# A transformer layer on one core: attention in even steps, token loads in small pieces

## What is computed

```python
h = x @ w_in                                  # split into q, k, v, z, b, a, c_q, c_kv, k_r
o_gdn = gated_delta_rule(q, k, v, g, beta)    # chunks of 64 tokens, 4 heads
for blk in range(S // Q_BLOCK):               # attention, 4 heads, keys up to the end of the block
    s = (einsum(q_nope, k_nope) + einsum(q_rope, k_rope)) * scale
    prob = softmax(where(mask, s, -inf))
    out = einsum(prob, v)
mix = concat([o_gdn, o_mla]) @ w_out
x = layer_norm(ALPHA * x + mix)
x = layer_norm(ALPHA * x + (silu(gate) * up) @ w_down)       # gate, up = split(x @ w_gate_up)
return x + sigmoid(x @ w_ple_gate) * (p_i @ w_ple)
```

## Time and profile before

| | us |
|---|---|
| median of 3 runs | 3401.8 (3395.01 to 3408.82) |
| the profiled execution, its time | 3407.16 |
| its span, first to last instruction | 3405.7 |
| attention, first matmul to the end of its last | 1101.6 to 1511.1 |
| op stage, first w_hi copy to the first matmul of feed_in | 1516.1 to 1744.6 |
| TensorE busy in the span | 3095.6 (91%) |
| mean granted TensorE clock | 0.958 |

### The profile page before, as it was taken

One profiled execution on the slowest core, in us unless ns is written; L12 is line 12 of the kernel. 1 busy time (PEld: TensorE's weight loads), 2 busy tenths in 40 slices (PEclk: granted clock), 3 DMA queues, 4 the chain that ended last, 5 costly groups with the idle time before them and its releaser, 6 DMA issues. The chain is left out here.

```text
span 3405.7 us, 45425 instructions
## 1 busy us (share of the span) xinstructions
PE 3095.6 (91%) x15074; PEld 2550.6 (75%) x15074; DVE 1641.7 (48%) x2713; ACT 1064.9 (31%) x2363; POOL 1115.6 (33%) x1245
## 2 busy tenths in 40 slices
PE   6999997768887897979879999989998999999898
PEld 5888885557776776868667888878887788887676
DVE  3653005446664554555576545675554433333333
ACT  2111004334434554542233333433333311111321
POOL 2322241165655866620045333453332000000122
PEclk9999998889988998999989999999999999999999
DMA  3212115412223211125624222232221532333433
GB/s 142 78 74 79 69 62 188 157 51 80 70 61 98 60 41 52 30 73 181 220 84 136 74 92 74 75 114 92 74 90 53 176 101 88 101 96 116 150 120 97
DMA packets 284042, 329.32 MB, mean 97 GB/s; under 512 B 32896, under 2 KB 224256, under 8 KB 279552
## 3 DMA queue, kind: packets, MB, share of 16 engines
q1 hardware_dynamic: 238248, 265.84, 24.6%
q0 software_dynamic: 12384, 45.09, 3.8%
q10 hardware_dynamic: 33280, 16.78, 1.7%
HBM read 210.73 MB, written 116.92 MB: 96 GB/s over the span
## 5 line engine op out<-in xcount | busy, mean ns | idle before, releaser
L2107 PE MATMUL ff_bank<-ff_x_hi,ff_w_lo 128*128 128x512 f32 x1240 | 488.2, 394 | 31.9 <-DVE ff_w_lo L2287 22.5
L2108 PE MATMUL ff_bank<-ff_x_lo,ff_w_hi 128*128 128x512 f32 x1240 | 487.0, 393 | 0.0
L2109 PE MATMUL ff_bank<-ff_x_hi,ff_w_hi 128*128 128x512 f32 x1240 | 486.6, 392 | 0.0
L2090 POOL TENSOR_TENSOR ff_w_sum<-ff_w_raw 128x512 f32<-128x512 f32 x210 | 299.3, 1435 | 495.7 <-DVE ff_w_lo L2287 439.3
L299 PE MATMUL in_h_ps<-in_x_hi,in_w_lo 128*128 128x512 f32 x704 | 276.6, 393 | 26.0 <-POOL in_w_lo L255 26.0
L2107 PEld LDWEIGHTS ff_bank<-ff_x_hi,ff_w_lo 128*128 128x128 f32 x1240 | 235.6, 190 | 84.0 <-DVE ff_w_lo L2287 25.3
L2497 PE MATMUL fd_acc<-fd_w_hi,fd_a_lo 128*128 128x512 f32 x704 | 279.8, 397 | 13.2 <-DVE fd_a_lo L2481 13.2
L2499 PE MATMUL fd_acc<-fd_w_hi,fd_a_hi 128*128 128x512 f32 x704 | 278.0, 395 | 0.0
L2498 PE MATMUL fd_acc<-fd_w_lo,fd_a_hi 128*128 128x512 f32 x704 | 278.0, 395 | 0.0
L301 PE MATMUL in_h_ps<-in_x_hi,in_w_hi 128*128 128x512 f32 x704 | 275.8, 392 | 0.0
L300 PE MATMUL in_h_ps<-in_x_lo,in_w_hi 128*128 128x512 f32 x704 | 275.8, 392 | 0.0
(11 more groups left out here) (383 smaller groups left out, 6640.6 us busy)
## 6 DMA issues: line engine op xcount, KB each, us to landing
ff_w_raw<-w_gate_up SPq DMA_DIRECT2D x44, 1024.0 KB, 5.1
scratch_hT<-in_out SPq DMA_DIRECT2D x22, 1024.0 KB, 3.9
fd_a_raw<-scratch_hid SPq DMA_DIRECT2D x176, 128.0 KB, 2.1
dr_qkv<-scratch_hT SPq DMA_DIRECT2D x16, 768.0 KB, 5.2
in_w_raw<-w_in POOLq DMA_DIRECT2D x22, 512.0 KB, 3.9
scratch_hid<-ff_first SPq DMA_DIRECT2D x44, 256.0 KB, 2.3
scratch_hid<-ff_second SPq DMA_DIRECT2D x44, 256.0 KB, 2.3
fd_w_raw<-w_down SPq DMA_DIRECT2D x22, 512.0 KB, 5.3
```

The lines of the kernel that those rows point to most:

```text
L2090: pool.tensor_tensor(w_sum[:, SUM_SLOT[m]], w_raw[:, b, one], w_raw[:, b, two], op).then_inc(w_sum_done, 1)
L2107: pe.matmul(acc, w_lo[:, wm, ws], x_hi[:, xm, k], start=first_mm, stop=False, skip_group_check=skip)
L2108: pe.matmul(acc, w_hi[:, wm, ws], x_lo[:, xm, k], start=False, stop=False, skip_group_check=skip)
L2109: return pe.matmul(acc, w_hi[:, wm, ws], x_hi[:, xm, k], start=False, stop=last_mm, skip_group_check=skip)
```

## The change

Attention is written without a loop, as 144 steps, one for each pair. Blocks of a head come in the order j = 7, 0, 6, 1, 5, 2, 4, 3. In step (n, p) TensorE transposes the pair two further on, also across blocks, multiplies pair p with v, and then does a share of the score groups of block n+3: of its G groups, those from G·p/pairs to G·(p+1)/pairs. Three blocks' scores are made before the first step. Four buffers of probabilities take the place of two (two of them half as long), three score banks the place of four, and two accumulators the place of one. The next head's pieces come at fixed steps, from step 2 to step 20 of a head; VectorE now copies the high part (`split_highs`, 60 copies in all: 36 single and 12 twice) and GpSimd makes the low part only. `HIGH_AT` puts the first head's last five pieces at the end of `delta_rule`.

```diff
+    ORDER = [j for m in range(NB // 2) for j in (NB - 1 - m, m)]
+    blocks = [(h, j) for h in range(HEADS) for j in ORDER]
+    LOOK, AHEAD = 3, 2
+    S_RING, T_RING, ACCS = 3, 3, 2
+    FIRST_PIECE, PIECE_STEPS = 2, 20
...
+        def steps():
+            every = [(n, p) for n in range(N) for p in range(pairs[n])]
+            for i, (n, p) in enumerate(every):
+                upto = min(i + AHEAD + 1, len(every))
+                turns, n_turned = every[n_turned:upto], upto
+                now, m = [], n + LOOK
+                if m < N:
+                    all_m = score_groups(m)
+                    now = all_m[len(all_m) * p // pairs[n]:len(all_m) * (p + 1) // pairs[n]]
...
+            for n, p, turns, now, ends, whole, left, pieces in steps():   # TensorE
+                for n1, p1 in turns:
+                    turn(n1, p1)
+                values(n, p)
+                for group in now:
+                    scores(*group)
...
+                if kind == 2:                                             # VectorE, split_highs
+                    reached(dve, split_low, count + 1 - 4)
+                    dve.tensor_copy(qr_hi[:], src)
+                    dve.tensor_copy(qr[b][ROPE:, ts], src[ROPE:]).then_inc(split_high, 1)
+                else:
+                    dve.tensor_copy((q_hi, k_hi, None, v_hi)[kind][b][:, ts], src).then_inc(split_high, 1)
...
+            for n, p, turns, now, ends, whole, left, pieces in steps():   # VectorE
+                for n1, p1 in turns:
+                    low(n1, p1)
+                if whole is not None:
+                    scales(whole)
+                for group in now:
+                    maximum(*group)
+                for h, m in pieces:
+                    split_highs(h, m)
+                if ends is not None:
+                    gaps(ends)
```

The token loads of the feed stage come as 16 pieces of 256 KB in place of four of 1 MB, both in the op stage and between the two passes of `feed_in`. In the op stage a weight load goes behind the first chunk load of tile 10 and of tile 11, and one token piece behind each chunk load of tiles 12 to 15:

```diff
+    def prepare_feed(sp, tp, t, c):
+        piece = tp.CH * (t - TILES) + c + 16
+        if piece >= 0:
+            feed_load_x(sp, ff, x1T, 0, piece)
+        elif c == 0:
+            sp.wait_ge(tp.w_lo_done, tp.K)
+            feed_load_w(sp, ff, a["w_gate_up"], t % 2, t % 2)
```

More of the change, by code:

```diff
@@ L1615, in attention @@
         out_done = s.sem("out_done")
-        out_free = s.sem("out_free")
-        stored = s.sem("stored")
+        stored = [s.sem(f"stored{b}") for b in range(2)]
         block = ctx.enter_context(nc.Block())
[L1619 to L1630, removed]
         def widths(j, tile):
@@ new lines, in steps @@
+        def steps():
+            every = [(n, p) for n in range(N) for p in range(pairs[n])]
+            n_turned, whole, left, count = 0, None, None, 0
+            for i, (n, p) in enumerate(every):
[5 more added lines that the diff above has]
+                    now = all_m[len(all_m) * p // pairs[n]:len(all_m) * (p + 1) // pairs[n]]
+                ends = m if m < N and p + 1 == pairs[n] else None
+                h, i0 = blocks[n][0], pair0[NB * blocks[n][0]]
+                pieces = [m for m in range(PIECES) if h + 1 < HEADS and i0 + FIRST_PIECE + PIECE_STEPS * m // PIECES == i]
+                yield n, p, turns, now, ends, whole, left, [(h + 1, m) for m in pieces]
+                whole, left = ends, n if p + 1 == pairs[n] else None
@@ L1748, in values @@
                 last.then_inc(pv_done, 1)
[L1750 to L1766 removed]
+            pe.wait_ge(const_sem, 2)
@@ L1768, in _ @@
+            for n in range(LOOK):
+                for group in score_groups(n):
+                    scores(*group)
[4 more added lines that the diff above has]
+                for group in now:
+                    scores(*group)
         @block.scalar
         def _(act):
[L1770 to L1778 removed]
@@ new lines, in out_copy @@
+            def out_copy(n):
+                act.wait_ge(pv_done, pair0[n + 1])
+                reached(act, stored[n % 2], 16 * (n // 2))
+                act.activation(out[:, n % 2], acc_ps[:, n % ACCS, 0:QB], ACT.Copy).then_inc(out_done, 1)
+            act.preload_act_table(ACT.Exp)
+            for n in range(LOOK):
+                for group in score_groups(n):
+                    exps(*group)
+                factors(n)
+            for n, p, turns, now, ends, whole, left, pieces in steps():
+                if left is not None:
+                    out_copy(left)
+                for n1, p1 in turns:
+                    high(n1, p1)
+                for group in now:
+                    exps(*group)
+                if ends is not None:
+                    factors(ends)
@@ new lines, in _ @@
+            for n in range(LOOK):
+                for group in score_groups(n):
+                    maximum(*group)
+                gaps(n)
+                scales(n)
+            for n, p, turns, now, ends, whole, left, pieces in steps():
+                for n1, p1 in turns:
+                    low(n1, p1)
+                if whole is not None:
+                    scales(whole)
+                for group in now:
+                    maximum(*group)
+                for h, m in pieces:
+                    split_highs(h, m)
+                if ends is not None:
+                    gaps(ends)
@@ new lines, in _ @@
+            for count in range(RAW):
+                load(count)
+            for n, p, turns, now, ends, whole, left, pieces in steps():
+                for h, m in pieces:
+                    if PIECES * (h - 1) + m + RAW < PIECES * (HEADS - 1):
+                        load(PIECES * (h - 1) + m + RAW)
+                if left is not None:
+                    store(left)
+                if (n, p) == (NB * (HEADS - 1) + 1, 0):
+                    sp.wait_ge(pv_done, pair0[NB * (HEADS - 1)])
+                    op.load_chunks(sp, mixed)
+                    op.load_weights(sp, w_out, range(op.first))
@@ L2025, in load_x @@
                 sp.wait_ge(x_lo_done, XP * p)
-                feed_load_x(sp, ff, xT, p)
+                for piece in range(16):
+                    feed_load_x(sp, ff, xT, p, piece)
             def load_w(f, b):
```

447 lines of the change are left out of this document (169 added, 278 removed).

## The result

The changed kernel takes **3368.0 us** (median of 8 runs, 3364.4 to 3376.6), the kernel before beside it 3396.3 us (8 runs, 3386.2 to 3408.8): ratio 0.9919, 95% interval 0.9906 to 0.9933, 28 us less. The forecast was 3345 us and 57 us less: the sign and the range (3308 to 3380) are right, the gain is half of what I worked out. The time lies outside the 3330 to 3360 that I had named as the forecast proper, and next to the 3369 of the rival *VectorE bounds the middle*. The profiled execution took 3365.1 us.

A forecast was written before the change was run, and what follows sets the result against it. TensorE was 91% busy, with some 89 us of attention's 409 lost to stalls from the order of work. Attention at 365 us (-44) and the op stage (-13) took 3401.8 to 3345 us, range 3308 to 3380.

The forecast's parts named there:

- VectorE bounds the middle: Rival: attention's piece copies cost their upper price, 45 us; attention 389 us, total 3369 us; chance 0.18.
- The unit costs: Attention: TensorE's unstalled need, 162.6 us for scores and 157.9 for pairs, together 320 us.
- (a): Attention: TensorE enters score groups from other work 79 times at 0.08 us, adding 6 us.
- (b): Attention's start: scale and first-values chain, twice not covered by other work, adding 5 us (bounds 3 and 9).
- (d): Start of heads 1 to 3: scaling of a 7-pair block late by about 1.5 us each, adding 4 us.
- (f): Attention: twelve steps with odd hitches, such as an accumulator or late piece before a head's first scores, adding 5 us.
- (c): Attention: pair's ScalarE copy stands behind the previous step's exponentials; 11 score runs at 0.4 us, adding 4 us.
- Attention, removed: Attention: the present stalls of 89 us go; steady pair rows, including the last twelve without scores, do not stall.
- (e): Attention: 60 copies moved to VectorE wait for GpSimd's instructions; adds 21 us over three heads (bounds 0 and 45).
- All hidden: Rival: VectorE's slack absorbs copy waits and late scaling and odd hitches vanish; attention 335, total 3315 us; chance 0.24.
- Slower: Rival: each of 60 copies meets a scaling instruction on TensorE's path, 132 us; attention 476, total 3455; chance 0.04.
- the hole stays: Rival, op stage: token pieces still get ahead of chunk loads, the hole only moves; 3358 us; chance 0.03.

The follow-up runs named there:

- e4: Changed kernel with pieces split in head 0 only, 40 of 60 pieces left out with their loads, copies and low parts: 3341.2 us, ratio 0.9828.
- e9: Changed kernel with each step's last exponential on ScalarE put behind the next step's high part, piece copies still on VectorE: 3342.4 us, ratio 0.9828.
- e7: Changed kernel with score groups at an even rate, 40 in 36 steps, and scale steps right behind a block's last group: 3393.0 us, ratio 0.9972.
- e10: Changed kernel with each step's last exponential behind the next high part and the 60 piece copies on ScalarE: 3326.0 us, ratio 0.9790.
- e11: Changed kernel with even score groups, piece copies on ScalarE, last exponential behind the next high part, pieces one step earlier: 3310.9 us, ratio 0.9753.
- e1: Changed kernel with attention's steps, rings and piece placing as before; only small token loads and op stage new: 3386.9 us, ratio 0.9949.
- e5: Changed kernel with delta_rule's old places for head 0's pieces: 3370.9 us, ratio 0.9911.
- e6: The kernel before, unchanged, run once more for its profile: 3393.3 us in one execution.
- e8: Changed kernel with even score groups and the 60 piece copies on ScalarE: 3402.0 us, ratio 1.0005.

## Why the prediction was half right

**Attention, sum.** The measured 396.6 us part into three. The pieces cost 38.6 us (the table of first steps; e4 gives 28.6 of it, for heads 1 and 2). ScalarE's order costs 23.5 us where there are no pieces: 6.2 in head 3 (after less e9), and by an estimate from that head's first steps and the other heads' last 14 (38.2 us in the changed kernel, 36.5 in e9) 5.8 in each other head. The rest is 334.5. Against the forecast's 365:

- The unit costs and (a), (b), (d), (f): 320 + 6 + 5 + 4 + 5 = 340 were forecast for what is now 334.5. As a total this nearly held; the parts were not measured one by one, and (d) alone is seen to be wrong: the wait for scaling is 0.2 us, not 4.
- **(c) is one term that was mis-sized**, with the sentence under "Attention, removed" that a steady row of pairs stalls nowhere "with the same ring and the same two pairs ahead". I priced the position of the pair's copy behind the exponentials only where the next two steps have no scores, 11 x 0.4 = 4 us. It also costs where a single step without scores follows, and more at each place: 23.5 us without any pieces, and 30.0 us with them (e9). The twelve pairs without scores, which I had called free of stalls, lose 2.0 us at their start. Where steps with one group follow each other (e7), the same position is the bound.
- **(e) is the other**: 21 us were forecast (bounds 0 and 45) and 38.6 measured. The mechanism was right (the copies end with GpSimd's instructions) and the mean too, by two errors that cancel. The sum was not: I set VectorE's busy time against TensorE's over all 22 steps (where 22 x 1.1 + 20 x 1.2 is 48, not 49), which takes it that a held copy is made up anywhere in the 22 steps, and I left out the clock. By differences taken in this order, 6.7 of the 38.6 us go with ScalarE's order (after less e9), 12.6 with the copies' place on VectorE (e9 less e10), 15.1 with the lumps and the late loads (e10 less e11, which also has the pieces one step earlier); 4.2 are left.
- The lumps had no term. I took spreading over a block's pairs as spreading; but the block three further on has the other size, so most of the groups fall on the few pairs of small blocks. e11 is 14.0 us shorter than e10, all of it in heads 0 to 2: the lumps cost only together with the pieces.

**The clock** I named only as a sign of being wrong (below 0.9). It was 0.93 in heads 1 and 2, and the longer busy time of TensorE is 6.5 of the 14.4 us that a head gains in e4. I had counted stalls by idle time alone.

**The rivals.** *VectorE bounds the middle of each head* gave 3369 us, one off the measured time. It was near in its price for the pieces (45 us, measured 38.6), but not all of that is VectorE's load, and its attention of 389 us is 7.6 short, since it has (c) at 4 us too. That the total came out all the same is luck: the kernel before had a median 5.5 us lower over eight runs than over the first three, and the op stage gave 1.9 us more. *All hidden* (attention 335) is what e11 nearly reached, by edits that the change did not have. *Slower* and *the hole stays* did not come.

**The op stage**: forecast 13 us, measured 14.9, and 15.6 in e1, just past the bound of 15. **delta_rule's end**: 0 forecast, 0 shown by e5. **The base**: the first profile of before held 14 us of slow delta_rule (e6); the sum was made relative to its total and scaled to the median, and attention's share was not touched by it.

**The signs**: scaling wait under 5 (0.2), copies' mean 0.7 to 1.2, and no wait above 2 us in tiles 12 to 15 came as written. The wait for low parts stayed above 25 (28.9), and a wait for score banks appeared (12.6 in all, the longest 3.1), close to what I had listed as a sign of being wrong. Head 3 was shorter than said (68.7, not 80), the others longer.

## What to carry to other kernels

When two in-order engines hand work to each other in both directions within a step, write down the cycle through both queues, entries that are only queued behind each other included, and compare its length with the bound engine's step. If it is longer, move one item past the other engine's next dependency (here the last exponential behind the next high part, 30 us) before spreading or rebalancing anything; until then a better balance can make it worse, as e7 and e8 show. Where one part of the kernel does the same work without the thing in question, as head 3 does without pieces, compare it with the others in the same profile: that gives a price that differences between runs, each taken with other limits in force, can hide. And read a difference between two profiles only after a second profile of the same kernel has shown how far a stage strays by itself.

## What the hardware showed that I had not expected

- A stall of 1.93 us was followed by 7 us at the lower level of TensorE's clock (0.52), and one of 2.05 us in e9 by none. Where the stalls recur, about as much again was lost in longer busy time (6.5 of 14.4 us a head in the changed kernel against e4).
- A VectorE operation of 6 elements, `at_gap` in SBUF, took 1.01 us in the mean and one of 8 elements 0.17; both read two operands in SBUF. It is the hold of the earlier trace rows: of the 24 operations 15 took 0.16 to 0.17 us with GpSimd idle, and nine took 1.28 to 1.30, started with one of GpSimd's low parts and ended 0.02 us after it.
- delta_rule took 12 to 14 us more in two of the three profiled executions with the old attention, and about 12 more in e9 with the new one: it goes with the execution, not with the kernel. The granted clock in delta_rule was 0.88 in these three and 0.90 and 0.91 in e6 and the changed kernel; whether the clock or the waits came first, no run here shows.
